# gMLP gating in a four-layer trunk: rows normalised by ACT, gated product and its parts kept in the spatial product's banks, matmul products one tile ahead, weights fetched ahead of the norm's rows

## The reference

```
def gmlp_mixer(h, w_in, ln_g, ln_b, w_s, b_s, w_out):
    z = gelu(h @ w_in)                       # (tokens, 4096)
    u, v = z[..., :2048], z[..., 2048:]
    v = layer_norm(v, ln_g, ln_b)            # over 2048
    # chunks of 128 tokens, 8 groups of 256 channels, w causal
    mixed = einsum('gts,bnsgc->bntgc', tril(w_s), v) + b_s
    return (u * mixed) @ w_out, v            # v of the sample rows is an output
```

## Time and profile before

| | us |
|---|---|
| median of 3 runs | 3565.93 (3565.59 to 3566.57) |
| the profiled execution, its own time | 3569.81 |
| its span | 3568.0 |
| PE busy in the span | 3238.6 (91%) |
| DVE, POOL, ACT busy | 1794.8, 1499.0, 484.0 |
| mean granted clock of PE | 0.952 of full speed |

### The profile page before, as it was taken

The page is one execution under the profiler, slowest core; times in us unless marked ns, Lnnn a source line. Parts: engine busy times, 40 slices in busy tenths (PEclk is TensorE's granted clock), DMA queues, the critical chain, the costliest instruction groups (busy, mean ns, idle before and its releaser), DMA issues.

```text
span 3568.0 us, 54595 instructions
## 1 busy us (share of the span) xinstructions
PE 3238.6 (91%) x22732; PEld 2970.4 (83%) x22732; DVE 1794.8 (50%) x2802; ACT 484.0 (14%) x1004; POOL 1499.0 (42%) x876
## 2 busy tenths in 40 slices
PE   5988799999888699999878979999998988899997
PEld 4878789999866489999875548899998988899997
DVE  3164664534677764533654446443343456644335
ACT  2210040000210130000311202200013100210001
POOL 2343435555466345455320013455544343355551
PEclk8999999999999899999987989999999999999998
DMA  5531244432221044432212113454322232123221
GB/s 202 203 98 57 75 171 137 145 127 78 74 59 36 17 171 136 148 125 83 64 40 80 44 42 107 139 164 129 101 78 61 66 90 65 53 84 89 78 84 56
DMA packets 450515, 343.83 MB, mean 96 GB/s; under 512 B 24936, under 2 KB 435936, under 8 KB 437965
## 3 DMA queue, kind: packets, MB, share of 16 engines
q1 hardware_dynamic: 443104, 333.59, 29.7%
q10 hardware_dynamic: 7165, 6.76, 0.7%
HBM read 335.77 MB, written 5.25 MB: 96 GB/s over the span
## 4 chain that ended last, share of the span: by engine, by line
issue 45%; POOL 22%; PE 16%; POOLq 10%; DVE 4%; SPq 2%; DVEq 1%; ACT 0%; DMA 0%; ACTq 0%
POOL w_lo L671 22%; PE pb L736 16%; POOLq L670 10%; DVE pb L2028 1%; SPq L634 1%; SPq L636 1%; SPq L638 1%; DVE a_lo L1592 0%; DVE xa L1735 0%; DVE full L2012 0%; DVE yc L2036 0%; PE pb L810 0%; DVE yc L2033 0%; DMA out_y_prompt<-yo 0%; DVE qaT L2163 0%
## 5 line engine op out<-in xcount | busy, mean ns | idle before, releaser
L669 POOL TENSOR_SCALAR w_hi<-w_raw 128x1024 fp32r<-128x1024 f32 (+2 forms) x416 | 442.4, 1064 | 1869.0 <-DMA w_raw<-in_ffn_w_up 424.8
L736 PE MATMUL pb<-h_hi,w_hi 128*128 128x288 f32 x3584 | 1083.7, 302 | 64.2 <-DVE h_lo L1762 21.8
L736 PE MATMUL pb<-h_lo,w_hi 128*128 128x288 f32 x3584 | 1069.6, 298 | 0.0
L736 PE MATMUL pb<-h_hi,w_lo 128*128 128x288 f32 x3584 | 1069.2, 298 | 0.0
L671 POOL TENSOR_TENSOR w_lo<-w_raw,w_hi 128x1024 fp32r<-128x1024 f32 (+2 forms) x416 | 972.4, 2338 | 62.4 <-issue 1.7
L736 PEld LDWEIGHTS pb<-h_hi,w_hi 128*128 128x128 f32 x3584 | 687.4, 192 | 118.9 <-issue 66.6
L736 PEld LDWEIGHTS pb<-h_lo,w_hi 128*128 128x128 f32 x3584 | 687.1, 192 | 0.3
L736 PEld LDWEIGHTS pb<-h_hi,w_lo 128*128 128x128 f32 x3584 | 686.2, 191 | 0.0
L736 PE MATMUL pb<-a_hi,w_hi 128*128 128x288 f32 x2176 | 649.7, 299 | 30.6 <-DVEq L2065 11.3
L736 PE MATMUL pb<-a_hi,w_lo 128*128 128x288 f32 x2176 | 644.6, 296 | 0.0
L736 PE MATMUL pb<-a_lo,w_hi 128*128 128x288 f32 x2176 | 644.5, 296 | 0.0
(11 more groups left out here) (274 smaller groups left out, 3227.4 us busy)
## 6 DMA issues: line engine op xcount, KB each, us to landing
ada_w<-in_ada_w SPq DMA_DIRECT2D x96, 1024.0 KB, 5.8
w_raw<-in_ffn_w_gate SPq DMA_DIRECT2D x88, 512.0 KB, 4.4
w_raw<-in_ffn_w_up SPq DMA_DIRECT2D x88, 512.0 KB, 3.7
w_raw<-in_gmlp_w_in SPq DMA_DIRECT2D x64, 512.0 KB, 5.2
w_raw<-in_ffn_w_down SPq DMA_DIRECT2D x64, 512.0 KB, 3.7
w_raw<-in_gmlp_w_out SPq DMA_DIRECT2D x32, 512.0 KB, 3.8
w_raw<-in_ffn_w_down SPq DMA_DIRECT2D x32, 384.0 KB, 3.2
w_raw<-in_conv_w_pw SPq DMA_DIRECT2D x24, 512.0 KB, 3.8
```

What stands on the lines that cost most here:

```text
L669: nc.gpsimd.tensor_scalar(w_hi[:, s, 0:w], w_raw[:, s, 0:w], 1.0, 1.0, ALU.mult, ALU.mult)
L736: return nc.tensor.matmul(out, lhsT, rhs, start=start, stop=stop)
```

## The change

The names that follow are as in the kernel before. Lines move by three (PE, SP) to about 50 (DVE).

- **ACT normalises**: DVE makes `vnb` = -mean/std once; ACT's Identity with scale `vrs` and bias `vnb` writes `vn` (`normalise_v`), for the next group behind the second Gelu of a group. DVE keeps gain and bias (`gains`), done for the next group behind the first tile of a group; for group 4 ahead of `down`.
- **The gated product stays in PSUM**: bias, product with `u_sb`, cast to `a_hi` and difference `a_lo` all read the aux banks, for a whole tile at a time (`gated_tile`). `u_sb` has two buffers, and ACT, not DVE, frees the banks of u.
- **Products one tile ahead**: PE makes the product of tile i+1 before the spatial product of tile i. The first output product waits for the last two tiles only in front of its last two k-tiles (`late_product`).
- **Loads**: SP loads weights up to three tiles ahead before it waits to load gain rows.
- The masks, transposes and copies of the spatial weights move up among the v products.
- `down` evacuates as `add_norm` does: the sample part in place in PSUM, without `smt`.

```diff
@@ SP
-                            load_to(plan.mark[l, ph, 2 * (g % 4)])
+                            load_to(plan.mark[l, 0, 8] + 4 if g == 4 else plan.mark[l, ph, min(2 * (g % 4) + 3, 8)])
                             sp.wait_ge(a_ready, 8 + a_n.n - 4)
@@ PE
+            def late_product(s, kt, late):
+                b = acc_bank()
+                for k in range(kt):
+                    if k in (0, kt - late):
+                        pe.wait_ge(a_ready, 8 + AR.n - 2 * (late if k == 0 else 0))
+                    for e, (w, a) in enumerate(((w_hi, a_hi), (w_hi, a_lo), (w_lo, a_hi))):
+                        last = mm(pb[:, b, 0:HALF], w[:, s, k * P:(k + 1) * P], a[:, k, 0:HALF],
+                                  k == 0 and e == 0, k == kt - 1 and e == 2)
+                last.then_inc(acc_ready, 1)
+                G.up()
...
+                    if (gg, tt) == (3, TT - 1):
+                        spatial_turns(l)
...
                 for ph in range(2):
+                    gated_u(8 * ph)
+                    for i in range(8 * ph, 8 * ph + 8):
+                        if i % 8 < 7:
+                            gated_u(i + 1)
+                        spatial(i)
                     AR.up(16)
                     if ph == 0:
-                        down(KT)
-                down_norm(KT)
+                        down(KT, late=2)
+                VN.up(GROUPS)
+                down_norm(KT, late=2)
@@ ACT
+                def normalise_v(g):
+                    if g == 0:
+                        act.wait_ge(vr_ready, j + 1)
+                    act.wait_ge(vo_done[g % 2], 16 + 16 * (VNA.n + g) // 2 - 8 * (g % 2))
+                    if g >= 2:
+                        act.wait_ge(a_ready, 8 + KA.n + 4 * (g - 1))
+                    for tt in range(TT):
+                        last = fn(vn[:, g % 2, tt, :], v_sb[:, tt, g * 256:(g + 1) * 256], ACT.Identity,
+                                  scale=vrs[:, tt:tt + 1], bias=vnb[:, tt:tt + 1])
+                    last.then_inc(vh_ready, 1)
+
+                normalise_v(0)
+                for g in range(GROUPS):
+                    for i in (2 * g, 2 * g + 1):
+                        for h in range(2):
+                            act.wait_ge(acc_ready, G.n + 1)
+                            if h == 0:
+                                act.wait_ge(acc_free, BANKS + G.n)
+                            if i >= 2 and h == 0:
+                                act.wait_ge(a_ready, 8 + KA.n + 2 * (i - 1))
+                            fn(u_sb[i % 2][:, half_cols(h)], pb[:, G.n % BANKS, 0:HALF], ACT.Gelu
+                               ).then_inc(sg_ready, 1)
+                            G.up()
+                        act.drain().then_inc(acc_free, 2)
+                        if i % 2 == 0:
+                            act.wait_ge(vn_ready, VNA.n + g + 1)
...
+                    if g + 1 < GROUPS:
+                        normalise_v(g + 1)
@@ DVE
+                def gains(g):
+                    gg = g % 2
+                    dve.wait_ge(gb_full[gg], GB[gg].up(48))
+                    dve.wait_ge(vh_ready, VO.n + g + 1)
+                    for n, op in enumerate((ALU.mult, ALU.add)):
+                        last_ = v.tensor_tensor(vn[:, gg], vn[:, gg],
+                                                gbt[:, gg, n, :].unsqueeze(1).to_broadcast([P, TT, 256]), op)
+                        dve.drain()
+                    dve.sem_inc(vn_ready, 1)
...
+                    dve.wait_ge(sg_ready, SG.up(2))
+                    parts = ((slice(0, SEQ), pp), (slice(SEQ, TOK), ps))
+                    for cols, src in parts:
+                        v.tensor_tensor(src, u_sb[q][:, cols], src, ALU.mult)
+                    dve.drain()
+                    for cols, src in parts:
+                        v.tensor_copy(a_hi[:, m, cols], src)
+                    dve.drain()
+                    for cols, src in parts:
+                        last_ = v.tensor_tensor(a_lo[:, m, cols], src, a_hi[:, m, cols].bitcast(F32), ALU.subtract)
+                    dve.drain().then_inc(a_ready, 2)
+                    dve.sem_inc(aux_free, 2)
+                    G.up(2)
+
+                gains(0)
+                for i in range(16):
+                    gated_tile(i)
+                    if i % 2 == 0 and i not in (6, 14):
+                        gains(i // 2 + 1)
+                    if i % 8 == 7:
+                        dve.wait_ge(acc_free, BANKS + G.n)
+                    if i == 7:
+                        gains(4)
                         down(2 * l)
```

More of the change, by code:

```diff
@@ L812, in transposes, with down @@
                 X.up()
-            def down(kt):
+            def late_product(s, kt, late):
[8 more added lines that the diff above has]
+                G.up()
+            def down(kt, late=0):
                 for m in range(KT):
@@ L818, in down @@
                     for h in range(2):
+                        if late and m == 0 and h == 0:
+                            late_product(s, kt, late)
+                            continue
                         pe.wait_ge(a_ready, 8 + AR.n - 1 + h)
@@ L918, in down_norm @@
                     for h in range(2):
+                        if late and m == 0 and h == 0:
+                            late_product(slots[0], kt, late)
+                            continue
                         pe.wait_ge(a_ready, 8 + AR.n - 1 + h)
@@ L979, in _, with spatial_turns @@
             ada_turn()
+            def spatial_turns(l):
+                pe.wait_ge(ws_ready, l // 3 + 1)
+                for q in range(2):
+                    transposes([(i * P, ws_raw[:, 4 * q + i, :]) for i in range(4)])
+                transposes([(g * NS, wss_raw[:, g, :]) for g in range(GROUPS)])
             def gmlp(l):
@@ new lines, in gated_u, with spatial @@
+                def gated_u(i):
+                    (s,) = take_units(1)
+                    for h in range(2):
+                        half_product(s, KT, h, (h_hi, h_lo))
+                def spatial(i):
+                    g, mt = divmod(i, 2)
+                    pe.wait_ge(vn_ready, VN.n + g + 1)
+                    b = aux_bank()
+                    for tt in range(4):
+                        last = mm(pb[:, b, tt * P:(tt + 1) * P], vn[:, g % 2, tt, mt * P:(mt + 1) * P],
+                                  one(wsT, g), True, True)
+                    last.then_inc(aux_ready, 1)
+                    X.up()
+                    b = aux_bank()
+                    mm(pb[:, b, 0:NS], vn[:, g % 2, 4, mt * P:(mt + 1) * P], one(wssT, g),
+                       True, True).then_inc(aux_ready, 1)
+                    X.up()
@@ L1822, in down_norm @@
                 SQ.up(7)
[L1824 to L1839, removed]
-                last_.then_inc(acc_free, 1)
-                G.up()
             def down(e):
@@ L1919, in gmlp @@
                 dve.drain()
-                for q in range(2):
-                    v.tensor_copy(wsT[:, 4 * q:4 * q + 4, :].rearrange("p g t -> p (g t)"), pb[:, aux(), :]
-                                  ).then_inc(aux_free, 1)
-                v.tensor_copy(wssT[:].rearrange("p g t -> p (g t)"), pb[:, aux(), :]).then_inc(aux_free, 1)
+                v.scalar_tensor_tensor(out=vnb[:], in0=bag[:, :, 0], scalar=-1.0, in1=vrs[:], op0=ALU.mult, op1=ALU.mult)
+                dve.drain().then_inc(vr_ready, 1)
@@ L1974, in gmlp @@
+                gains(0)
[7 more added lines that the diff above has]
+                        gains(4)
                         down(2 * l)
+                VO.up(GROUPS)
+                for n in range(2):
+                    dve.wait_ge(vo_done[n], 16 + 8 * VO.n)
@@ L1976, in _ @@
+                down_norm(2 * l, ffn_first)
             VV, VO = Tally(), Tally()
```

129 lines of the change are left out of this document (37 added, 92 removed).

## The result

The changed kernel takes 3474.19 us (median of 4, 3471.47 to 3477.19) against 3565.76 for the kernel before (median of 4): a ratio of 0.9745, 95% interval 0.9733 to 0.9757. The profiled execution took 3477.19 us for a span of 3475.4, at a mean granted clock of 0.962.

A forecast was written before the change was run, and what follows sets the result against it. PE's waits for vn in the gated phases of layers 0 and 3 were the bound. 79.9 + 13.5 - 2 = 91.4 off 3569.8 gives 3478.4 profiled, 3.9 less for the median: 3475 us, range 3463 to 3500.

The forecast's parts named there:

- The wait for vn, 0: Inside the four gated phases of layers 0 and 3, PE's steady wait for the normalised group falls to 0.
- The cover of 3 to 7 us: Time by which vn is ready before PE needs it: 3 us at worst, 7 as a rule.
- The stall at an end, 4.0: At each phase's end, PE idles 4.0 us in the first output product, waiting for DVE's two last tiles.
- E - 0.9: When DVE starts tile 6; E is the end of a phase's last spatial product.
- The clock behind it, 2 us in all: Extra slow-clock loss behind the four end stalls: 2 us taken, between bounds of 0 and 5.6.
- the 22.3 us of slow matmuls: Part of the old phases' 96.0 us loss: matmuls at 1.2 instead of 2.4 GHz, put behind 16 waits.
- The 1.4 it took for an end: Slow-matmul loss counted behind each of 16 waits, used for the clock's upper bound at the four ends.
- the saving of 79.9: Four gated phases of layers 0 and 3 fall from 335.15 to 255.3 us, stalls at their ends included.
- Ahead of phase 0, 13.5: Moving masks, transposes and copies among the v products saves 13.5 us before phase 0 of layers 0 and 3, at worst 10.7.
- Loads, 0: With weights loaded ahead of gain rows, neither weights nor gain rows arrive late: 0 us.
- ScalarE's rows, 0: Normalising on ACT instead of DVE costs 0, being covered; if engine time counted, 22 us back, giving 3497.
- The unknown, 0 of 0 to 17: Whether differences reading PSUM and SBUF stretch beside GpSimd in a phase's two last tiles: 0 taken, up to 17 us.

The follow-up runs named there:

- e10: Changed kernel, but DVE makes gain and bias of the next group behind a group's second tile instead of its first; 3494.63 us, ratio 0.9798.
- e8: Changed kernel, but each spatial product right behind its own product u, no product ahead; 3482.30 us, ratio 0.9759.
- e1: Changed kernel, but a phase's first output product waits for all a_hi tiles before it starts; 3485.71 us, ratio 0.9778.
- e2: Changed kernel, with six k-tiles of both halves of the first output unit ahead of the wait for the last two tiles; 3456.43 us, ratio 0.9698.
- e3: Changed kernel, with tile 6's spatial product ahead of product 7, the first output product waiting for the last tile alone; 3460.40 us, ratio 0.9703.
- e5: Changed kernel, but DVE normalises the rows, five operations a group ahead of gain and bias, instead of ACT; 3483.13 us, ratio 0.9760.
- e9: Changed kernel, but the gated product is written to u_sb in SBUF, and a_hi and a_lo made from there; 3494.60 us, ratio 0.9805.
- e11: Changed kernel, but DVE normalises rows, spatial products follow their own products u, and the gated product goes through u_sb; 3502.21 us, ratio 0.9824.
- e4: Changed kernel, with tile 6's spatial product ahead of product 7 and seven k-tiles of both output halves before the last tile's wait; 3456.01 us, ratio 0.9698.
- e6: Changed kernel, but masks, transposes and copies of the spatial weights behind the v products again; 3485.17 us, ratio 0.9769.
- e7: Changed kernel, but SP's loads in the old order except for group 4; 3552.65 us, ratio 0.9961.

## Why the prediction was right

It said 3475; it is 3474.2. The single executions spread over 5.7 us, so the last microseconds of that agreement are luck; the steps are what counts:

- **The wait for vn, 0:** right. The four phases take 59.83, 59.74, 59.75 and 59.75 us with no idle time. The cover of 3 to 7 us was real, and it comes from several parts: without DVE's new place 12 waits come back (e10), without the product in hand 9 (e8), each of 0.7 to 5 us.
- **The stall at an end, 4.0:** 4.04 in each. The working (two tiles of 3.65 from E - 0.9, less 2.4 of matmuls) also gave the 6.5 of e1, 1.64 of e2, 0.9 of e3 and 1.3 of e8, each within 0.1. It doesn't give those of e5 (1.3 to 3.8), e10 (2.5 to 3.5), e9 (5.2 to 8.0) and e11 (6.3 to 7.3), where operations on SBUF stretch or the last spatial product comes late.
- **The clock behind it, 2 us in all:** the output product of phase 0 takes 50.97 at full clock (e4). Less the stall it took 53.98 and 52.57 in after, so 3.0 and 1.6 for the slow matmuls, against 52.50 - 50.97 = 1.5 behind the 2.56 of before. Behind phase 1, up to the first `part` matmul, it is 38.16 at full clock (e4) and 39.94 and 41.16 in after, so 1.8 and 3.0, against 1.5 too. 3.3 us more in all, within the 0 to 5.6 and over the 2; and uneven. The prediction read one thing wrong here: its windows end at the first `a_hi` matmul, so the 22.3 us of slow matmuls stand behind the 12 waits for `vn` and at the phases' starts, at most 1.9 for each on average, and none behind the 4 waits at the ends. The 1.4 it took for an end was near the 1.5 all the same, and the saving of 79.9 doesn't rest on it.
- **Ahead of phase 0, 13.5:** in layer 0 the gap fell from 10.8 us to 1.27, in layer 3 to nothing. Undone in e6 it is worth 11 to 13.
- **Loads, 0:** right for this order. The prediction gave the new order no credit, since it asked only whether it could be late; e7 shows that, with the product in hand, the rest is worth little without it. With products one tile ahead the weights are wanted one tile sooner, and the old order has them 7 us behind that.
- **ScalarE's rows, 0:** right in that e5 doesn't gain; whether it loses is open. The Trainium skill, page "ScalarE: Activation LUTs", section "Rules for kernel authors", would give this work to VectorE, and the case goes the other way, if at all.
- **The unknown, 0 of 0 to 17:** right, and this is the term with the most at stake. `a_lo<-pb,a_hi` stays at 693 ns, and e9, the same kernel with the SBUF form, loses 20.4 us. The Trainium skill, page "SBUF — State Buffer", section "SBUF: two separate sides", says that a VectorE instruction with at most one SBUF input, outside the 2-port modes, doesn't contend with GpSimd; the rows from PSUM agree. The cast from SBUF has one SBUF input as well and stretched to 2335 ns in e9; in which mode it ran no row shows.

Sum: 3568.0 - 3475.4 = 92.6 us in the profile for 91.4 predicted. The four phases with their stalls give 79.9 of it, as predicted.

What stays open: whether e5 and e8 really lose, since their intervals touch that of the changed kernel; what the new order of loads is worth without the product in hand; and what vn's place in DVE's order, whole tiles and the early release of the banks are worth each, since none was put alone into the kernel before and only the place was undone alone (e10). The stretch itself was seen only where GpSimd and DVE met by chance; it wasn't measured by itself.

## What to carry to other kernels

Cost a change of order in legs from one fixed event and ask of each wish who else wants something sooner by it: the product in hand moved the wish for weights, and with the old order of loads most of the gain was gone. Where a stall at a seam is a known chain, put enough independent work ahead of it (here the second half of the same output unit, 2.4 us): it took 18 us more off, 10 of them the stall and the rest slow matmuls, since the clock no longer fell. Where DVE and GpSimd work side by side, look at maxima and not at medians.

## What the runs showed of the hardware

DVE's casts, differences and row operations between SBUF buffers take up to six or seven times their undisturbed time while GpSimd splits weights: 128x256 rows 401 to 2630 ns (e5), 128x288 casts 309 to 2245 and differences 457 to 2621 (before). In the rows looked at, the stretched operation ends with the split beside it, whatever its width: in e9 a difference of 64 columns, 217 ns alone, took 2362 and ended within 0.1 us of a split of 2.87 us. Operations with one operand or the source in PSUM stay within a few ns of 692 for 512 columns, beside such splits. ACT's 128x256 rows stay within 584 to 602 ns, and half of the 16 groups of them lie beside a split. I had expected the difference to stretch by 2.2 us, and not that rows and casts with a single SBUF source would; in the kernel before, five rows of 1.7 us took 6.61 ahead of the longest wait for vn.
